# A router's VectorE chain in another order: choice masks first, ranks straight into the column table, the work list's casts in front of the columns

## The reference

```python
scores = jax.nn.sigmoid((t @ w_router).astype(jnp.float32))
_, eidx = lax.top_k(scores + router_bias.astype(jnp.float32), TOP_K_EXPERTS)   # 8 of 64
g = jnp.take_along_axis(scores, eidx, axis=1)
g = g / jnp.sum(g, axis=-1, keepdims=True) * ROUTED_SCALE
...                              # tokens sorted by expert, in blocks
def expert_block(args):
    e, toks, gs = args
    xb = t[toks]
    return swiglu(xb, w1[e], w3[e], w2[e]) * gs[:, None]
...
routed = jax.ops.segment_sum(out.reshape(rows, D), row_tok, num_segments=n_tok)
shared = swiglu(t, ws1, ws3, ws2)
return (routed + shared).reshape(B, S, D)
```

## Time and profile before

| | |
|---|---|
| time of the profiled execution | 1019.35 us |
| its span (first to last instruction) | 1017.5 us |
| PE busy | 968.3 us, 95% |
| DVE busy | 750.4 us, 74% |
| ACT busy | 580.1 us, 57% |
| POOL busy | 418.1 us, 41% |
| granted TensorE clock, mean | 0.994 |
| router to first expert block | about 620 to 653 us |

### The profile page before, as it was taken

How to read it: one execution, slowest core, us unless ns; L and a number is a source line. 1 busy time by engine, 2 the same in 40 slices (tenths; PEclk the granted TensorE clock), 3 DMA queues, 4 the chain that set the end, 5 groups by cost and what they waited for, 6 DMA issues and landing times. The chain is left out here.

```text
span 1017.5 us, 16364 instructions
## 1 busy us (share of the span) xinstructions
PE 968.3 (95%) x5072; PEld 775.5 (76%) x5072; DVE 750.4 (74%) x1322; ACT 580.1 (57%) x896; POOL 418.1 (41%) x373
## 2 busy tenths in 40 slices
PE   7999999999999899999979998899999999999996
PEld 6778877778766676778768888678787787778874
DVE  4678888768854454457686755498898988898988
ACT  4555655455433533243535532588887888888875
POOL 5164453223300000023223321466777767777675
PEclk9999999999999999999989999999999999999998
DMA  9877676776844416336233321988888888888883
GB/s 309 290 255 260 223 259 231 259 241 196 288 159 146 139 51 239 106 113 198 105 132 117 126 83 51 364 336 314 346 315 340 345 312 344 320 326 343 325 325 146
DMA packets 79430, 238.58 MB, mean 234 GB/s; under 512 B 12876, under 2 KB 19077, under 8 KB 66066
## 3 DMA queue, kind: packets, MB, share of 16 engines
q1 hardware_dynamic: 66146, 196.60, 53.0%
q0 software_dynamic: 12656, 40.91, 11.6%
q10 hardware_dynamic: 576, 0.41, 0.1%
HBM read 235.58 MB, written 2.16 MB: 234 GB/s over the span
## 5 line engine op out<-in xcount | busy, mean ns | idle before, releaser
L1919 PE MATMUL bank<-w_hi,a_hi 128*128 128x512 f32 (+2 forms) x512 | 205.9, 402 | 10.7 <-DVE w_lo L1333 9.0
L1919 PE MATMUL bank<-w_hi,a_lo 128*128 128x512 f32 (+2 forms) x512 | 197.2, 385 | 0.0
L1919 PE MATMUL bank<-w_lo,a_hi 128*128 128x512 f32 (+2 forms) x512 | 196.9, 385 | 0.0
L1333 DVE TENSOR_TENSOR w_lo<-ring,w_hi 128x1024 fp32r<-128x1024 f32 (+2 forms) x134 | 155.5, 1182 | 49.6 <-ACT w_hi L1016 44.8
L1016 ACT ACTIVATE w_hi<-ring 128x1024 fp32r<-128x1024 f32 (+2 forms) x140 | 141.3, 1024 | 78.3 <-PE bank L1919 74.6
L1732 DVE TENSOR_TENSOR up_lo<-raw_weights,up_hi 128x1024 fp32r<-128x1024 f32 x120 | 146.3, 1255 | 0.0
L1181 ACT ACTIVATE up_hi<-raw_weights 128x1024 fp32r<-128x1024 f32 x136 | 135.9, 1054 | 0.0
L1919 PEld LDWEIGHTS bank<-w_hi,a_hi 128*128 128x128 f32 x512 | 96.8, 189 | 39.1 <-issue 20.6
L809 POOL TENSOR_SCALAR mean_squares<-mean_squares 128x8 f32<-128x8 f32 (+2 forms) x32 | 9.9, 310 | 279.9 <-ACT logits L969 199.2
L1919 PEld LDWEIGHTS bank<-w_hi,a_lo 128*128 128x128 f32 x512 | 96.6, 189 | 19.9
L1919 PEld LDWEIGHTS bank<-w_lo,a_hi 128*128 128x128 f32 x512 | 97.0, 189 | 18.5 <-issue 1.4
(11 more groups left out here) (284 smaller groups left out, 1904.1 us busy)
## 6 DMA issues: line engine op xcount, KB each, us to landing
raw_weights<-in_w_dram SPq DMA_DIRECT2D x102, 1024.0 KB, 7.0
ring<-in_w_in_dram SPq DMA_DIRECT2D x58, 1024.0 KB, 6.0
merged<-in_w_ada_dram POOLq DMA_DIRECT2D x96, 256.0 KB, 4.2
ring<-in_w_out_dram SPq DMA_DIRECT2D x8, 1024.0 KB, 5.8
ring<-in_w_branch_dram SPq DMA_DIRECT2D x6, 1024.0 KB, 4.8
bias<-rel_rows SPq DMA_DIRECT2D x40, 128.0 KB, 4.9
ring<-in_ws_dram SPq DMA_DIRECT2D x2, 1024.0 KB, 4.9
merged<-in_x_dram SPq DMA_DIRECT2D x2, 512.0 KB, 5.2
```

What stands on the lines that cost most here:

```text
L1333: dve.tensor_tensor(w_parts[1][:, 2 * p:2 * p + 2, 0:w], view(JOB[it[1:3]], kind)[:, 2 * p:2 * p + 2, :], w_parts[0][:, 2 * p:2 * p + 2, 0 ...
L1919: mm = pe.matmul(ps[:, 0:wide], a_parts[za][:, k, t * P:(t + 1) * P], w_parts[zw][:, k, 0:wide], start=start, stop=stop)
```

## The change

Four edits, all in the router's chain and what waits for it.

1. The mask is written twice straight into `taken`, ahead of the sums, and `sel` is no longer turned into a mask. The two copies go.
2. The ranks of a token tile go straight into `pcol` (the two casts L1699 go). Only tile 0's are made before the list's places; tile 1's follow behind `order`.
3. The two casts of the work list come in front of the gates' columns, and the number of blocks is written last. SP waits for `work_ready` at 1 ahead of block 0's weights, and for 3 behind them.
4. On PE, two of the shared expert's steps move from ahead of the product that counts kinds to behind the list's product.

```diff
-            sp.wait_ge(S("work_ready"), 3)
+            sp.wait_ge(S("work_ready"), 1)
...
             load_down(0, load_up(0, 0))
+            sp.wait_ge(S("work_ready"), 3)
             n_work = sp.value_load(work[0:1, 0:1], min_val=0, max_val=MAX_WORK)
...
-                    chain(dve.tensor_scalar(sel[:, :, :], sel[:, :, :], TAKEN / 2, None, ALU.is_lt))
-                    chain(dve.tensor_tensor(sig[:, :, :], sig[:, :, :], sel[:, :, :], ALU.mult))
+                    for j in range(2):
+                        dve.tensor_scalar(taken[:, :, N_EXP * j:N_EXP * j + N_EXP], sel[:, :, :], TAKEN / 2, None, ALU.is_lt)\
+                           .then_inc(S("taken_ready"), 1)
+                    dve.wait_ge(S("taken_ready"), 1)
+                    chain(dve.tensor_tensor(sig[:, :, :], sig[:, :, :], taken[:, :, 0:N_EXP], ALU.mult))
...
-                    for j in range(2):
-                        ins = dve.tensor_copy(taken[:, :, N_EXP * j:N_EXP * j + N_EXP], sel[:, :, :])
-                        ins.then_inc(S("taken_ready"), 1)
...
-                        dve.tensor_scalar(ranks[:, t, :], ranks[:, t, :], -FAR, None, ALU.add)\
+                        dve.tensor_scalar(pcol[:, 0:NV, 4 * t + 3], ranks[:, t, :], -FAR, None, ALU.add)\
                            .then_inc(S("ranks_ready"), 1)
+
+                    rank_column(0)
                     dve.wait_ge(S("places_counted"), 1)
...
-                    dve.wait_ge(S("ranks_ready"), NT)
+                    rank_column(1)
+                    dve.wait_ge(S("list_product"), 1)
+                    dve.tensor_copy(work[0:1, 1:1 + NV], y_b[1][0:1, 0:NV]).then_inc(S("work_ready"), 1)
+                    dve.tensor_scalar(work[0:1, 1 + NV:1 + 2 * NV], y_b[1][0:1, NV:2 * NV], float(NV), None, ALU.add)\
+                       .then_inc(S("work_ready"), 1)
...
-                        chain(dve.tensor_copy(pcol[:, 0:NV, 4 * t + 3], ranks[:, t, :]))
...
-            up(wv, 0, 1, range(0, 2))
...
-            up(wv, 0, 1, range(2, 6))
+            up(wv, 0, 1, range(0, 4))
...
-            up(wv, 0, 1, range(6, KT))
+            up(wv, 0, 1, range(4, KT))
```

More of the change, by code:

```diff
@@ L1670, in _, with rank_column @@
                     dve.tensor_tensor(kinds[:, 1:2], used[:, :], kinds[:, 0:1], ALU.subtract).then_inc(S("used_ready"), 1)
-                    for t in range(NT):
+                    dve.wait_ge(S("taken_ready"), 2)
+                    def rank_column(t):
                         chain(dve.tensor_tensor(ranks[:, t, :], y_b[0][:, NV * t:NV * t + NV],
@@ L1698, in _ @@
                         chain(dve.tensor_tensor(lo, gate, hi.bitcast(F32), ALU.subtract))
-                        chain(dve.tensor_copy(pcol[:, 0:NV, 4 * t + 3], ranks[:, t, :]))
                     chain(dve.tensor_scalar(n_blocks[:, :], place[0:1, 2:3], 2.0, -1.0, ALU.mult, ALU.add))
+                    dve.wait_ge(S("ranks_ready"), NT)
+                    dve.wait_ge(S("work_ready"), 2)
                     dve.scalar_tensor_tensor(out=work[0:1, 0:1], in0=place[0:1, 3:4], scalar=place[0:1, 2:3],
                                              in1=n_blocks[:, :], op0=ALU.add, op1=ALU.max).then_inc(S("work_ready"), 1)
[L1703 to L1706, removed]
             def take_tokens(i, r, found):
```

## The result

The changed kernel took 1026.45 us (median of 20 runs, 1024.41 to 1029.72), the kernel before 1023.63 us (median of 20 runs, 1021.55 to 1028.11). The ratio is 1.0031 with a 95% interval of 1.0021 to 1.0041: slower by 0.3%, and the medians differ by 2.8 us. The time lies in the forecast's range and within 0.5%, but the sign is the other one: a gain of 1.2 us was forecast. That the forecast's 1026.7 us all but meets the measured 1026.45 us is luck. It started from 1027.86 us, the median of the first three runs, which stood 4.2 us above that of all 20. From 1023.63 us the same sum gives 1022.4 us. The profiled execution of the changed kernel took 1026.34 us with a span of 1024.5 us.

The account below looks back on a forecast made before the run. PE bounds the loop, so block 0's start decides: columns issued at 633.9 us + 5.35 + 1.26 puts PE at 640.5 us, 1.2 us earlier. 1027.86 us becomes 1026.7 us, range 1021.5 to 1031.5 us, within 0.5% (90%).

Parts of the forecast that it names:

- What bounds: Second half: the loop runs at PE's pace, losing some 2.3 us to other waits; the first block's start sets the end.
- the margin of 1.17 us: PE's shared-expert work is only 1.00 + 0.17 us shorter than the path to `pick`; called the least that could be recovered.
- The masks, the rank column, the list: Router's chain up to the list: counts 1.11 us earlier, copy of the places and list's product 1.89 us earlier.
- Casts and columns: DVE from the places to the last cast: 4.39 us, so columns issued 1.7 us earlier, weights 3.4 us earlier.
- how long block 0's columns take to land: Block 0's columns from issue to `pick`: 5.35 us, where it was 4.88 us; bounds 4.88 and 10.8 us.
- Rival 1: Landing of block 0's columns: weights delay it to 7.9 us, PE goes on 1.35 us later, 1029.2 us; 35%.
- rival 2: Same landing at 10.8 us: PE idles 6.4 us and the clock falls, together +6.25 us, 1034.1 us; 4%.
- The early weights bring nothing: Block 0's weights: ACT rounds them first at 643.81 us without waiting for a transfer, so issuing them earlier gains nothing.
- The paragraph on the page "DMA: Bandwidth & Descriptors" of the Trainium skill: Block 0's columns would stand behind weight transfers like block 1's, 7.9 us: shared descriptor generators, per-packet turns, completions after earlier writes.

Follow-up runs that it names:

- e2: The kernel before with only the early weights (list's casts between the two tiles' columns, SP waits for 1, then 3): 1028.72 us, ratio 1.0055 to before.
- e3: The changed kernel with 14 instead of 4 filling matmuls ahead of the pick product: 1024.68 us, ratio 1.0014 to before.
- e5: The changed kernel with SP waiting for 3 between w1 and w3, meant to have one of three weight transfers early: 1027.68 us, ratio 1.0042 to before.
- e4: The kernel before once more, unchanged, for a second profile: 1023.61 us, ratio 1.0006 to before.
- e7: As e1, with SP also waiting for block 0's columns to land before it issues block 0's weights: 1024.46 us, ratio 1.0005 to before.
- e8: e1 without the four filling matmuls ahead of the pick product: 1023.14 us, ratio 0.9981 to before.
- e10: e1 run again, unchanged: 1021.49 us, ratio 0.9964 to before.
- e1: The changed kernel with SP waiting for `work_ready` at 3 again ahead of block 0's weights: 1021.55 us, ratio 0.9971 to before.
- e6: The changed kernel with block 0's and 1's columns issued by GpSimd's software queue instead of ScalarE, weights early: 1024.69 us, ratio 1.0015 to before.
- e11: The kernel before with SP's read of the number of blocks moved ahead of block 0's weights: 1024.03 us, ratio 0.9988 to before.
- e9: e1 with SP's read of the number of blocks moved ahead of block 0's weights: 1022.25 us, ratio 0.9969 to before.

## Why the prediction was wrong

- **What bounds: right, to about a microsecond.** The first block's start was the thing to look at. The loop took 342.10 us against 342.01 us in the two first profiles, but up to 346.25 us in the others, and PE went without a gap from the pick product to turning the rows, only slower. One word was wrong: with PE's own work unmoved, the margin of 1.17 us is the most that could be recovered, not the least.
- **The masks, the rank column, the list: right.** Forecast gains of 1.11, 1.89 and 1.89 us up to the counts, the places and the list's product; measured 1.11, 1.89 and 1.85 us.
- **Casts and columns: nearly right.** The columns' issue was to come 1.7 us earlier and came 1.51 us earlier (r + 13.65 against 15.16 us). The second rank column took 1.01 us up to the casts (631.91 to 632.92 us), where the sum had 0.78 us; that is the difference. The weights came 3.51 us earlier (3.4 us forecast), so their lead was 1.56 us and not 1.3 us.
- **The failed step** is the one on "how long block 0's columns take to land". I took 5.35 us, block 1's time without what I took for its wait for its own predecessor. Measured 7.42, 7.60, 7.27 and 7.60 us (the changed kernel, e2, e3, e5). With it PE was to go on at r + 20.1 us (640.5 us in the profile of before), and it went on at r + 22.33 us. Block 1's 7.9 us had been the right row as it stood. None of its packets moved for 3.6 us after its issue, and block 0's columns, with no predecessor, now wait 3.9 us just so. Two other runs tell the two waits apart, which the prediction could not. In e4 block 0's columns had landed after 1.8 us, and block 1's still took 7.5 us. In e7, with no weights in the way, block 1's landed in 1.8 us behind the same predecessor. So the wait was for the weights, and the wait for the predecessor, which I took off, was not there to take off. The seven packets that I read as getting through were the tail of a transfer that had been ahead of the weights; the same seven show in e8 and e10. Why the first packet of a later transfer waits so long stays open.
- **Rival 1 had the place and the point, and no price for the clock.** It gave PE's delay as 1.35 us, measured 1.03 us; its landing time of 6.55 us was passed. The clock is the second term that was put too low: I charged it only to rival 2, for an idle time of 6.4 us; with 3.46 us idle it fell too, and it costs 3.2 us in the profile, three times the delay itself. My own row showed full speed for 3.77 us of idle time and the low level afterwards, and rival 1's idle time, 3.5 us by my own numbers (643.06 less 639.6 us), was too near to that to leave it out.
- **"The early weights bring nothing": right for this kernel, and too mild.** They are the whole loss. e1, which differs from the changed kernel in that one wait, is 0.3% to 0.4% faster than before, as the shorter chain promised. But that the weights were in time before holds only where the columns are slow. With quick ones ACT waited for the weights, 0.78 us in the kernel before (e4) and 0.86 us in e1.
- **The paragraph on the page "DMA: Bandwidth & Descriptors" of the Trainium skill,** section "Queues, rings and completion order", pointed the right way. Of its parts, the DMA engines' turns between the queues show in the trace from 640 us on (one column packet to about one weight packet), and they don't by themselves give the 3.9 us before the first turn. Whether a packet of the trace is what the page calls a packet, several descriptors together, is not shown. Shared descriptor making is not all that delays the columns, since GpSimd's queue waited as well (e6). No run here tests the rule on completions.

Not settled: the profiles put the loss of the stage at 4.2 us (5.0 us against the second profile of before, 31.82 us), the medians at 2.8 us. Each profile is one execution. In the 13 profiles the router starts anywhere from 619.67 to 624.66 us, and the loops from the first to the last block differ from 342.0 to 346.3 us. In e7 and e11 1.5 and 1.7 us of that are the fallen clock of the first block; I tried nothing that would tell the rest. Whether the columns are quick or slow by chance is a small part: it moved the first block's start by 0.74 us in the kernel before and by 0.64 us in e1's.

The version that beats both is e1: the changed kernel with SP's wait at 3, at 0.9971 and 0.9964 of before in two samples. e9, with the gap on top, is as good (0.9969).

## What to carry to other kernels

Before you move large transfers forward, look for a small one on the critical path that will then be issued behind them, even a microsecond or two later. Here the 4 KB of columns cost the kernel more than the shorter chain gave. Issue the small one first, but don't hold the large ones back longer than that, for they become the bound in their turn (e7, e11). When a wait of PE grows to 2.5 us or more, price the clock behind it, not only the wait: in this case waits of 2.57 to 3.74 us were followed by the lower level, and those of 1.00 to 2.08 us for `pick` were not. And if the trace has one instance of just the thing that you must price, take its time whole before you take it apart.

## What the runs showed of the hardware

- The transfer of block 0's columns, 144 packets, took 1.96 to 2.08 us from issue to the instruction that waits for it where its packets moved ahead of the weights' (e4, e7, e9, e11). Behind two or three megabytes of weights it took 7.3 to 7.6 us, and none of its packets moved for 3.4 to 4.0 us after the issue (changed kernel, e2, e3, e5).
- With 0.42 to 0.44 us between its issue and that of the weights it took 1.97, 3.19, 4.88, 5.03 and 5.07 us in five profiles (e4, e1, before, e10, e8), and with 0.99 us it took 2.00 and 2.08 us (e9, e11).
- The granted clock fell 3.2 us after PE had stopped in the changed kernel (641.31 to about 644.5 us), 3.8 us after in the earlier case and only 1.8 us after in e2 (642.93 to about 644.75 us). In e6 it fell when PE had gone on again, after 2.57 us of idle time. So the length of the idle time alone does not tell when it falls.
- In the changed kernel it was at its lower level for 6.7 us, of which PE worked 6.4 us; in e6, e7 and e11 it was there for some 3.4 us.
- A software-queue transfer of the same 4 KB showed 32 packets where ACT's showed 144 (e6).
